# Layer norm of a convolution branch: four tiles and their squares added on VectorE, one product with ones for each sum

## The reference

```python
def conformer_conv(ga, gb, dw_w, dw_b, ln_g, ln_b, w_pw2):
    u = ga * jax.nn.sigmoid(gb)
    u = causal_dwconv(u, dw_w, dw_b)
    uf = u.astype(jnp.float32)
    mu = jnp.mean(uf, axis=-1, keepdims=True)
    var = jnp.mean(jnp.square(uf - mu), axis=-1, keepdims=True)
    un = (uf - mu) * lax.rsqrt(var + EPS) * ln_g.astype(jnp.float32) + ln_b.astype(jnp.float32)
    return jax.nn.silu(un).astype(u.dtype) @ w_pw2
```

## Time and profile before

| | us |
|---|---|
| median of the runs shown (3 runs, 2673.57 to 2676.76) | 2674.05 |
| the profiled execution | 2674.82 |
| its span | 2673.0 |
| PE busy in it | 2579.5 |
| DVE busy in it | 1544.0 |
| POOL busy in it | 1065.7 |

### The profile page before, as it was taken

The page is one execution under the profiler, slowest core; times in us unless marked ns, Lnnn a source line. Parts: engine busy times, 40 slices in busy tenths (PEclk is TensorE's granted clock), DMA queues, the critical chain, the costliest instruction groups (busy, mean ns, idle before and its releaser), DMA issues.

```text
span 2673.0 us, 35546 instructions
## 1 busy us (share of the span) xinstructions
PE 2579.5 (97%) x12484; PEld 1992.9 (75%) x12484; DVE 1544.0 (58%) x2510; ACT 1145.3 (43%) x1984; POOL 1065.7 (40%) x430
## 2 busy tenths in 40 slices
PE   8999999999999899999999999997999999999998
PEld 6867666788888688676677888885887776887776
DVE  6138747853223670576488334227688766787765
ACT  3344544433222343454535233235337554347554
POOL 4432223344445344222133544442446612447612
PEclk9999999999999999999999999999999999999999
DMA  5221112222223242111122322221223211223211
GB/s 200 94 83 48 56 46 78 82 95 94 94 94 104 77 124 92 66 57 47 48 93 81 109 96 94 94 100 58 88 93 126 72 41 48 94 95 125 73 41 56
DMA packets 64203, 224.27 MB, mean 84 GB/s; under 512 B 7888, under 2 KB 8016, under 8 KB 64080
## 3 DMA queue, kind: packets, MB, share of 16 engines
q1 hardware_dynamic: 63504, 221.06, 24.2%
q10 hardware_dynamic: 576, 1.57, 0.2%
HBM read 216.57 MB, written 2.10 MB: 82 GB/s over the span
## 4 chain that ended last, share of the span: by engine, by line
PE 82%; DVE 7%; DVEq 4%; ACT 3%; issue 2%; POOL 1%; ACTq 0%; DMA 0%; SPq 0%
PE bank L396 23%; PE bank L398 22%; PE bank L397 22%; PE bank L545 3%; PE bank L572 3%; DVEq L2241 2%; PE bank L558 2%; POOL w_lo L454 1%; PE bank L548 1%; PE bank L820 1%; PE bank L1169 1%; PE bank L794 1%; DVE ffn_sum L1691 1%; PE bank L803 1%; PE bank L1220 0%
## 5 line engine op out<-in xcount | busy, mean ns | idle before, releaser
L454 POOL TENSOR_TENSOR w_lo<-w_raw,w_hi 128x1024 fp32r<-128x1024 f32 x404 | 1014.7, 2519 | 1582.7 <-ACT w_hi L405 1576.7
L396 PE MATMUL bank<-x_hi,w_hi 128*128 128x512 f32 x2112 | 856.7, 406 | 29.8 <-DVE x_lo L2470 10.6
L398 PE MATMUL bank<-x_hi,w_lo 128*128 128x512 f32 x2112 | 829.4, 393 | 0.0
L397 PE MATMUL bank<-x_lo,w_hi 128*128 128x512 f32 x2112 | 828.4, 392 | 0.0
L405 ACT ACTIVATE w_hi<-w_raw 128x1024 fp32r<-128x1024 f32 x400 | 419.5, 1055 | 416.3 <-PE bank L398 355.3
L396 PEld LDWEIGHTS bank<-x_hi,w_hi 128*128 128x128 f32 x2112 | 399.8, 189 | 133.7 <-issue 32.6
L398 PEld LDWEIGHTS bank<-x_hi,w_lo 128*128 128x128 f32 x2112 | 399.7, 189 | 86.2
L397 PEld LDWEIGHTS bank<-x_lo,w_hi 128*128 128x128 f32 x2112 | 400.4, 190 | 78.3 <-issue 2.9
L396 PE MATMUL bank<-rhs_hi,w_hi 128*128 128x512 f32 x624 | 246.5, 395 | 6.1 <-DVE rhs_lo L1593 6.1
L397 PE MATMUL bank<-rhs_lo,w_hi 128*128 128x512 f32 x624 | 244.5, 392 | 0.0
L398 PE MATMUL bank<-rhs_hi,w_lo 128*128 128x512 f32 x624 | 244.2, 391 | 0.0
(11 more groups left out here) (409 smaller groups left out, 3203.2 us busy)
## 6 DMA issues: line engine op xcount, KB each, us to landing
w_raw<-w SPq DMA_DIRECT2D x404, 512.0 KB, 3.4
work<-proj SPq DMA_DIRECT2D x60, 64.0 KB, 2.0
ln_in<-x SPq DMA_DIRECT2D x4, 512.0 KB, 7.3
out<-residual SPq DMA_DIRECT2D x8, 256.0 KB, 2.1
p_raw<-p ACTq DMA_DIRECT2D x2, 512.0 KB, 3.5
constants<-con SPq DMA_DIRECT2D x1, 455.0 KB, 10.3
cos<-cos SPq DMA_DIRECT2D x1, 256.0 KB, 10.4
sin<-sin SPq DMA_DIRECT2D x1, 256.0 KB, 10.3
```

Source lines behind the costliest of these rows:

```text
L396: nc.tensor.matmul(out, wh, xh, start=first, stop=False)
L397: nc.tensor.matmul(out, wh, xl, start=False, stop=False)
L398: S.last = nc.tensor.matmul(out, wl, xh, start=False, stop=last)
L454: S.nc.gpsimd.tensor_tensor(S.wl[s][:, :], S.raw[s][:, :], S.wh[s][:, :].bitcast(F32), ALU.subtract).then_inc(S.lo_ready[s], 1)
```

## The change

The change gives the sums over the four tiles to DVE. Behind the taps DVE now waits until PE has turned the gate logits and v (`bvt_ready`, a wait that stood there before, behind the memset), adds the four tiles of the convolution in three additions into `lnstd` (the memory of vw), with a drain after each, and the last signals `dw_done`; the memset goes. The gates come behind. PE makes one product with ones of that sum in place of four.

For the variance DVE adds the squares into `lnsq[0]`, one addition behind each of the rotations 1, 2 and 3, each after the wait for its square; the third signals the new semaphore `cl_added`. PE waits for that one and makes one product in place of four. All additions are of two SBUF tiles of 128x512 float32.

```diff
--- before.py
+++ after.py
@@ -308,6 +308,7 @@
     S.cl_mean = sem("cl_mean")
     S.cl_d = sem("cl_d")
     S.cl_sq = sem("cl_sq")
+    S.cl_added = sem("cl_added")
     S.cl_var = sem("cl_var")
     S.cl_std = sem("cl_std")
     S.cl_y = sem("cl_y")
@@ -1900,9 +1901,7 @@
             cmp1(B_CMPV + q, 1, q, S.ps[0])
         pe.wait_ge(S.bank_free[B_ZC[2] % SLOTS], BF(L, B_ZC[2]) + 1)
         pe.wait_ge(S.dw_done, L + 1)
-        for t in range(4):
-            m = nc.tensor.matmul(S.ps[1][:, :], S.ones[:, :], seq(S.cacc, t), start=(t == 0), stop=(t == 3))
-        m.then_inc(S.cl_mean, 1)
+        nc.tensor.matmul(S.ps[1][:, :], S.ones[:, :], S.lnstd[:, :], start=True, stop=True).then_inc(S.cl_mean, 1)
         dense(B_ZC[3])
         dense(B_ZL[0])
 
@@ -1928,10 +1927,8 @@
         pe.wait_ge(S.lru_gate, L * 4 + 4)
         for q in range(4):
             if q == 2:
-                for t in range(4):
-                    pe.wait_ge(S.cl_sq, L * 4 + t + 1)
-                    m = nc.tensor.matmul(S.X[1][:, :], S.ones[:, :], S.lnsq[t][:, :], start=(t == 0), stop=(t == 3))
-                m.then_inc(S.cl_var, 1)
+                pe.wait_ge(S.cl_added, L + 1)
+                nc.tensor.matmul(S.X[1][:, :], S.ones[:, :], S.lnsq[0][:, :], start=True, stop=True).then_inc(S.cl_var, 1)
             cmp1(B_CMPK + q, 0, q, S.X[0])
         dense(B_ZL[1])
         rot(5)
@@ -2246,9 +2243,13 @@
             for t in pair:
                 tap(CONV_K - 1, t, seq(S.cacc, t))
             dve.drain()
-        nc.vector.memset(S.tick[:, 28:29], 0.0).then_inc(S.dw_done, 1)
-
         dve.wait_ge(S.bvt_ready, L * 3 + 3)
+        total = S.lnstd[:, :]
+        for t in range(1, 4):
+            m = nc.vector.tensor_tensor(total, total if t > 1 else seq(S.cacc, 0), seq(S.cacc, t), ALU.add)
+            dve.drain()
+        m.then_inc(S.dw_done, 1)
+
         nc.vector.tensor_scalar(S.gate[:, :].rearrange("p (b c) -> p b c", b=QB),
                                 S.X[2][:, :].rearrange("p (b c) -> p b c", b=QB)[:, :, 0:3 * B_HEADS], 1.0, 0.5,
                                 ALU.add, ALU.mult).then_inc(S.gl_done, 1)
@@ -2293,6 +2294,10 @@
             stt(out=seq(S.cacc, t), in0=S.ps[1][:, :], scalar=-2.0, in1=seq(S.cacc, t), op0=ALU.mult, op1=ALU.add).then_inc(S.cl_d, 1)
         for n in range(1, 5):
             rope(n)
+            if n < 4:
+                dve.wait_ge(S.cl_sq, L * 4 + n + 1)
+                m = nc.vector.tensor_tensor(S.lnsq[0][:, :], S.lnsq[0][:, :], S.lnsq[n][:, :], ALU.add)
+        m.then_inc(S.cl_added, 1)
 
         dve.wait_ge(S.lru_gate, L * 4 + 4)
         stt(out=S.lri[:, :], in0=S.lri[:, :], scalar=1.0, in1=S.xc[:, :], op0=ALU.add, op1=ALU.mult).then_inc(S.xc_free, 1)
```

## The result

| | before | after |
|---|---|---|
| median, us | 2674.05 | 2688.89 |
| lowest to highest of the runs | 2672.98 to 2678.71 (5) | 2688.52 to 2692.99 (5) |
| the profiled execution | 2674.82 | 2688.89 |
| its span | 2673.0 | 2687.1 |

The ratio is 1.0055, with an interval of 1.0043 to 1.0066. The forecast was 2683.3 in a range of 2673 to 2688; the kernel is slower, as forecast, but by 14.8 us and not by 9.3, and 0.9 us beyond the end of the range.

The account below looks back on a forecast made before the run. TensorE, busy 97% of the span, was taken to bound the kernel. First layer +7.3 and second layer +2.0 summed to +9.3 us, giving 2683.3 us in a range of 2673 to 2688.

Parts of the forecast that it names:

- rotation: TensorE's second rotation waits for the gates, now behind the mean's additions: +4.3 us first layer, +0.3 second.
- the clock's term: First layer: granted clock falls to 0.50 after two idle times of 5 us and more; one loss counted, +2.0 us.
- product of the mean: Four products of TensorE for the mean become one: -2.6 us in each layer.
- rotation 4: Fourth rotation product waits for VectorE's rotation 2, late among GpSimd's splits: +1.1 us first layer, +2.6 second.
- LRU gates hold TensorE: First layer: GpSimd's late LRU splits leave TensorE at +2.1, not +1.7; second: late squares hold ScalarE's gates, -1.0, not -2.3.
- variance, with its clock and the split behind it: Variance product waits for the third addition of squares (5.6 us first layer, 1.7 second), up to the next dense unit.
- weights of a later unit: Second layer: VectorE's LRU product delays ScalarE's tanh, so a later weight split comes 3.6 us late: +2.3 us.
- The adds start at 2399.75: Second layer: mean's additions end about 2402.2 and the rotation starts at 2402.5 instead of 2402.18, +0.3 us.
- the variance add (wait 1.7): Second layer: TensorE waits 1.7 us for the variance addition; next dense unit at 2452.3 instead of 2452.61.
- adds find gaps: Rival: VectorE wins the races with GpSimd, variance saving swallowed by the weight split; -2 to +5 us, chance 0.34.
- The third: Rival: TensorE's saving arrives, twelve products less (10.3 us) minus 4.3 at the first rotation; -6 us, 2668, chance 0.06.
- the collisions that cascade: Main case: VectorE additions and GpSimd splits hold each other up in both layers; +5.4 to +14 us, at +9.3, chance 0.60.

Follow-up runs that it names:

- gates_first: Changed kernel with VectorE writing the gates ahead of the three additions of the mean; 2684.82 us against 2675.23 for the kernel before, ratio 1.0032.
- var_only: Kernel before with only the variance's additions and its one product, the mean as before; 2676.23 us against 2674.93, ratio 1.0004.
- mean_only: Kernel before with only the mean's additions ahead of the gates and its one product; 2676.95 us against 2674.93, ratio 1.0012.
- no_adds: One product each for mean and variance, of the first tile alone, without additions; 2673.11 us against 2674.93 for the kernel before, ratio 0.9990.
- after_pad24: Changed kernel with twelve pairs of memset and drain in an idle time of VectorE, first layer; 2686.01 us, 1.0038 to the kernel before.
- pad_second: Kernel before with two pairs of memset and drain on VectorE in the second layer, behind the last tap loop; 2678.77 us, single run.
- pad_first: Kernel before with two pairs of memset and drain in an idle time of VectorE in the first layer; 2677.63 us, single run.

## Why the prediction was right and where it failed

The mechanism was right: VectorE, made late by collisions with GpSimd, holds TensorE at the rotation and at the variance product. The first layer's sum was right too, +7.5 against +7.3, but in part by luck. Its large terms came as forecast. The rotation waited 5.29 us (1.03+4.3=5.33 forecast). The third addition of squares ended at 2050.49; the forecast 2052.7, moved by the 2.26 us that this execution was ahead, is 2050.4. The wait at the variance product was 4.0 and not 5.6 us, since TensorE had lost 2.0 us to the lowered clock behind the rotation and came so much later. That is how the clock's term was argued: one loss is taken off a later wait, the other stays. Three smaller terms were off and cancelled: the product of the mean gave 1.5 us and not 2.6, as 0.8 went into a wait for a weight split, and the losses forecast at the LRU gates and at rotation 4 (0.4 and 1.1) did not come.

The second layer failed: +7.8 against +2.0. All terms are in us of TensorE's lateness; the forecast's clock term for the first layer, +2.0, was for both idle times together and is put behind the rotation here:

| term | first layer, forecast | measured | second layer, forecast | measured |
|---|---|---|---|---|
| rotation | +4.3 | +4.3 | +0.3 | +2.4 |
| clock behind it | +2.0 | +2.0 | 0 | +1.7 |
| product of the mean | -2.6 | -1.5 | -2.6 | -2.5 |
| LRU gates hold TensorE | +0.4 | 0 | +1.3 | +0.4 |
| rotation 4 | +1.1 | 0 | +2.6 | +1.1 |
| variance, with its clock and the split behind it | +2.1 | +2.3 | -1.9 | +4.7 |
| weights of a later unit | 0 | +0.4 | +2.3 | 0 |
| sum | +7.3 | +7.5 | +2.0 | +7.8 |

Two steps carry the miss. The first is "The adds start at 2399.75": they started 2.2 us later than the rest of the kernel was, because the last pair of taps ran slower. No row of before could show that, and the prediction had assumed in silence that code put behind a loop leaves the next layer's loop as it is. The slack of 2.2 us at this place was just used up by the three additions, so all of the loop's lateness fell on TensorE. The second is the term "the variance add (wait 1.7)": it was 5.4. In the first layer I had laid each addition against GpSimd's row of splits; for the second I had taken the lateness as a sum of single hold-ups. In the trace the last two instructions with two SBUF inputs ahead of that product, rotation 3's addition and the third addition of squares, each ran beside a weight split and took 2.54 and 2.82 us for 0.69. A third, smaller one hangs on these two: I took no clock loss in the second layer, as no idle time of 5 us was forecast there, and behind the rotation alone it was 1.7 us. One term was charged that did not come in the changed kernel: the late weights, +2.3. TensorE was itself too late to wait for them. In `gates_first`, where it was not, they came, in both layers (waits of 2.0 us each).

Of the rivals, the second ("adds find gaps") fits `var_only` (1.3 us); `mean_only` has its total (2.0 us) but not its way, for its rotation waits 5.3 us as with a collision. The third fell with `no_adds`. The first, the collisions that cascade, is what the runs show at the variance product; the slow tap loop is no part of it. The result lay at its worst end (14.8 us, where it had +14), and the range had cut that off at 2688.

Whether the remaining 1.8 us behind the second layer's stage belong to the change is open: the clock is lowered in the attention in after and in `after_pad24`, but in `pad_second`, which does nothing for the sums, too (2.4 us there). It may be a matter of where the clock happens to fall, but no run shows that.

## What to carry to other kernels

Before you give TensorE's sums to VectorE, count the instructions of VectorE that read two SBUF tensors against GpSimd's in the same stretch: here each addition that met one cost up to 2.2 us more than its 0.69, and a running sum kept in PSUM did not pay this. When a wait is moved away, as by the gates written first, follow the late engine to its next users: here the loss came back 80 us later at a weight split. Test the halves of a change together as well as alone, since the room that hides one half can be what the other needs (2.0 and 1.3 us became 14.8). And when code is added ahead of a loop, read that loop's pace again in the new trace, in later layers too.

## What the hardware showed that I had not expected

- The pace of a loop of VectorE hangs on how many instructions stand ahead of it: the same 58 took 49.27, 49.5, 50.2 or 51.5 us, with 0 to 32 instructions added ahead of them; in `pad_first` and `pad_second`, where the same four stood ahead of the loop or behind it, 51.47 and 49.30.
- An addition with one input in PSUM and one in SBUF runs in 0.70 us beside a split of GpSimd that runs its undisturbed 2.39.
- A wait of TensorE of about 2 us can be followed by a lowered clock, and need not be. Behind the 2.2 us at the second layer's rotation in after the mean is 0.71 (2408 to 2412), behind the 1.96 us at the weight split in `gates_first` it is 0.50. But behind a wait of 2.3 us at rotation 4 of the same kernel's second layer it is 1.00, and so it is behind the 1.0 us at its first layer's rotation:

```profile
2408.00:2412.00 4.00, 2.99 (x7) 1.85 (x8) 3.86 (x4) 0.37 (x1) 2.36 (x1) 0.71 0.09 10
```

```profile
2447.00:2451.00 4.00, 2.42 (x15) 1.89 (x16) 3.93 (x5) 3.64 (x5) 1.26 (x2) 1.00 0.68 238
2451.00:2455.00 4.00, 2.58 (x16) 1.79 (x15) 4.00 (x3) 2.12 (x2) 4.00 (x2) 1.00 0.15 23
```
